# Emptying PSUM banks before the next rounding, splitting DVE's scans, and taking roots of row variances on GpSimd

## The reference, cut to what matters

```python
gq_l, gk_l, gv_l, gr_l, gaf_l, gab_l, dq_l, dk_l, dv_l = split(h_l @ w_in, IN_OFFSETS)   # and of h_c
la_f = log_sigmoid(gaf @ w_a_up_f + b_a_f) / 16      # forward gates; la_b backward
b = cumsum(la)                                        # what the scans compute
...
x_new = x + g1 * mix_l                                # output jobs out0..out3
h2_l = rms_norm(x_new, norm2_w) * (1 + sc2) + sh2
x_new = x_new + g2 * conv_ffn(h2_l, ...)              # jobs downa0..3 and downb0..3
kv = rmsnorm(mem, mem_norm_g) @ w_mem_kv              # jobs km, vm
h = rmsnorm(x, norm_g) @ w_in                         # second layer
out = rmsnorm(x + o @ w_out, final_norm_g)            # jobs o20..o23, then the end
```

## Time and profile before

| | us |
|---|---|
| median of three runs | 2324.34 (2324.21 to 2324.67) |
| the profiled execution | 2324.98 |
| its span, first to last instruction | 2323.2 |
| PE busy | 2240.4 (96% of the span) |
| DVE busy | 1485.7 (64%) |
| ACT busy | 1038.5 (45%) |
| POOL busy | 47.3 (2%) |

### The profile page before, as it was taken

How to read it: one execution, slowest core, us unless ns; L and a number is a source line. 1 busy time by engine, 2 the same in 40 slices (tenths; PEclk the granted TensorE clock), 3 DMA queues, 4 the chain that set the end, 5 groups by cost and what they waited for, 6 DMA issues and landing times.

```text
span 2323.2 us, 37359 instructions
## 1 busy us (share of the span) xinstructions
PE 2240.4 (96%) x15465; PEld 2010.0 (87%) x15465; DVE 1485.7 (64%) x2116; ACT 1038.5 (45%) x1429; POOL 47.3 (2%) x61
## 2 busy tenths in 40 slices
PE   5899999999999999989999999999999999999997
PEld 2577777899888999779999988999978898999986
DVE  3346766387476478777888855566665644576664
ACT  3134343354555643344444433444454534454444
POOL 3000000021000000000000000000000000000000
PEclk9899999999999999999999999999999999999999
DMA  9956766454444578866778655555545566544454
GB/s 364 369 163 197 230 210 197 145 151 146 127 137 129 187 243 280 293 230 206 227 243 260 225 190 190 183 185 183 185 165 196 166 189 201 170 128 137 129 198 145
DMA packets 249738, 458.75 MB, mean 197 GB/s; under 512 B 18995, under 2 KB 43889, under 8 KB 248160
## 3 DMA queue, kind: packets, MB, share of 16 engines
q1 hardware_dynamic: 246496, 442.47, 58.7%
q0 software_dynamic: 2496, 9.69, 1.1%
q10 hardware_dynamic: 576, 4.19, 0.5%
HBM read 454.20 MB, written 2.10 MB: 196 GB/s over the span
## 4 chain that ended last, share of the span: by engine, by line
PE 82%; DVE 7%; ACT 3%; DMA 3%; DVEq 2%; issue 2%; SPq 1%; ACTq 0%
PE psum L648 73%; DVE fast L1921 2%; PE psum L625 2%; DVE sbuf L1973 2%; ACT fast L1324 1%; DMA sbuf<-in_w_ada 1%; PE psum L1157 1%; DVEq L1972 1%; PE psum L904 1%; PE psum L959 1%; PE psum L719 1%; DVE fast L1941 1%; DMA sbuf<-in_w_up 1%; PE psum L978 1%; PE psum L1187 1%
## 5 line engine op out<-in xcount | busy, mean ns | idle before, releaser
L648 PE MATMUL psum<-fast,fast 128*128 128x256 f32 (+1 forms) x13424 | 2034.2, 312 | 20.6 <-DVE fast L1921 14.4
L648 PEld LDWEIGHTS psum<-fast,fast 128*128 128x128 f32 x13424 | 1848.6, 191 | 195.4 <-issue 46.6
L1921 DVE TENSOR_TENSOR fast<-sbuf,fast 128x1024 fp32r<-128x1024 f32 (+5 forms) x685 | 784.0, 1152 | 678.5 <-ACT fast L1324 671.2
L1324 ACT ACTIVATE fast<-sbuf 128x1024 fp32r<-128x1024 f32 (+4 forms) x689 | 682.1, 998 | 1046.0 <-PE psum L648 911.5
L1973 DVE SCALAR_TENSOR_TENSOR sbuf<-sbuf,sbuf 128x512 f32<-128x512 f32 x210 | 157.8, 751 | 18.3 <-issue 0.5
L1324 ACT ACTIVATE sbuf<-psum 128x512 f32<-128x512 f32 (+4 forms) x193 | 85.6, 469 | 79.9 <-PE psum L648 33.3
L625 PE MATMUL psum<-sbuf,sbuf 128*128 128x128 f32 (+2 forms) x349 | 58.7, 284 | 22.3 <-DMA sbuf<-in_consts 10.5
L625 PEld LDWEIGHTS psum<-sbuf,sbuf 128*128 128x128 f32 (+2 forms) x349 | 42.7, 145 | 33.0 <-DMA sbuf<-in_consts 10.5
L1941 DVE TENSOR_TENSOR fast<-sbuf,fast 128x512 fp32r<-128x512 f32 (+1 forms) x61 | 53.4, 876 | 4.5
L1689 ACT ACTIVATE sbuf<-psum,sbuf 128x256 f32<-128x256 f32 x88 | 44.2, 552 | 0.0
L2352 DVE SCALAR_TENSOR_TENSOR sbuf<-psum,sbuf,sbuf 128x255 f32<-128x255 f32 x88 | 38.5, 478 | 3.6 <-issue 0.4
(11 more groups left out here) (263 smaller groups left out, 962.6 us busy)
## 6 DMA issues: line engine op xcount, KB each, us to landing
sbuf<-in_w_ada SPq DMA_DIRECT2D x192, 512.0 KB, 4.9
sbuf<-in_w_up SPq DMA_DIRECT2D x176, 512.0 KB, 4.4
sbuf<-in_w_in SPq DMA_DIRECT2D x154, 512.0 KB, 3.8
sbuf<-in_w_down SPq DMA_DIRECT2D x88, 512.0 KB, 4.3
sbuf<-in_w_gate SPq DMA_DIRECT2D x64, 512.0 KB, 3.6
sbuf<-in_w_out SPq DMA_DIRECT2D x64, 512.0 KB, 4.8
sbuf<-in_w_proj_gla SPq DMA_DIRECT2D x16, 512.0 KB, 4.7
sbuf<-in_w_proj_diff SPq DMA_DIRECT2D x16, 512.0 KB, 5.9
```

What stands on the lines that cost most here:

```text
L648: last = mm(out, lhsT, rhs, start=first and key not in opened, stop=end, skip_group_check=True)
L1324: return A(out, in_, ACT.Copy, scale=scale)
L1921: last = tt(lo, raw, hi.bitcast(F32), ALU.subtract)
```

## The change

Four edits. (1) In gv0 and gv1, ACT rounds all but the last chunk of its steps, copies the four banks out, and rounds the last one then. (2) DVE's eight scans per direction are issued as four and four, with a step of the job between them; the second direction thereby begins a step later. (3) In the output and down jobs each of the two token tiles is multiplied and at once added; in out3 the last residual chunk is computed after that. (4) Four roots of row variances leave ACT: POOL computes x to the power -0.5 for norm2, mem, norm3 and the final norm. The other three, of the first norm and of the two low-rank norms, stay on ACT. POOL writes the exponent once, makes one power in advance, and its queue holds these operations between its DMAs. ACT's early Ln goes in three places.

```diff
@@ gpsimd
+            def rsqrt(x, before):
+                pool.wait_ge(S("variance_ready"), before + 1)
+                nc.gpsimd.tensor_tensor(x, x, small[:, 116:118], ALU.pow).then_inc(S("rsqrt_done"), 1)
             pool.wait_ge(S("diff_pv_done"), 8)
             pool.dma_start(g1b, dram["b_ada"][0:1, 2 * D:3 * D].to_broadcast([P, D])).then_inc(S("spread_bias"), 16)
+            pool.memset(small[:, 116:118], -0.5)
+            pool.memset(small[:, 118:120], 1.0)
+            pool.drain()
+            nc.gpsimd.tensor_tensor(small[:, 118:120], small[:, 118:120], small[:, 116:118], ALU.pow)
...
             pool.wait_ge(S("x1_slices"), 8)
             pool.dma_start(g2b, dram["b_ada"][0:1, 5 * D:6 * D].to_broadcast([P, D])).then_inc(S("spread_bias"), 16)
+            rsqrt(small[:, 58:60], 1)
+            rsqrt(small[:, 66:68], 2)
             pool.wait_ge(S("mem_ready"), 8)
...
             pool.dma_start(pev[0:32, :], dram["cmp_pe_v_2"]).then_inc(S("cmp_loaded"), 16)
+            rsqrt(small[:, 58:60], 3)
             pool.wait_ge(S("mixed2"), 8)
...
             pool.wait_ge(S("gain_loaded"), 16)
+            rsqrt(small[:, 58:60], 6)
@@ scalar
-            def steps(name):
-                for g in st.job[name]:
-                    round_chunk(st.nth[g] + 2)
+            def steps(name, left=0):
+                n = len(st.job[name]) - left
+                for q, g in enumerate(st.job[name]):
+                    if q < n:
+                        round_chunk(st.nth[g] + 2)
                     next(side, None)
...
             for j in range(2):
-                steps(f"gv{j}")
+                steps(f"gv{j}", 1)
                 for t in range(4):
                     src, emptied = filled(f"gv{j}", t)
                     copy(gv[:, t, 512 * j:512 * j + 512], src).then_inc(emptied, 1)
+                round_chunk(st.nth[st.job[f"gv{j}"][-1]] + 2)
...
-                if n == 3:
-                    logarithms_next()
...
-            rsqrt(small[:, 58:60])
...
-            rsqrt(small[:, 58:60])
-            act.drain()
+            act.wait_ge(S("rsqrt_done"), 7)
@@ vector
                             last = v.tensor_tensor_scan(dst[:, p, 1:257], C("ones")[:, 0:1].to_broadcast([P, T]),
                                                        zb[:, p, lc * T:(lc + 1) * T], 0.0, ALU.mult, ALU.add)
+                        if p == 1:
+                            yield
                     last.then_inc(S("gates_summed"), 1)
...
                     stt(otmp[:, 2 * (n % 2) + t, :], src, 0.5, gain[:, c], ALU.mult, ALU.mult).then_inc(emptied, 1)
-                dve.drain()
-                for t in range(2):
+                    dve.drain()
                     tt(x1[:, t, c], x1[:, t, c], otmp[:, 2 * (n % 2) + t, :], ALU.add).then_inc(S("x1_slices"), 1)
...
             for n in range(4):
-                steps(f"out{n}")
+                steps(f"out{n}", n // 3)
                 add_rows(f"out{n}", n, g1b, "g1_kept")
+            rest_chunk(st.nth[st.job["out3"][-1]] + 2)
```

More of the change, by code:

```diff
@@ L1319, in _ @@
             A = nc.scalar.activation
-            roots = 0
             side = iter(())
@@ L1349, in filled, with rsqrt @@
                 return bank(BANKS[name][i]), S(f"bank_emptied{BANKS[name][i]}")
[L1351 to L1354, removed]
+            def rsqrt(v, before):
+                act.wait_ge(S("variance_ready"), before + 1)
                 A(v, v, ACT.Ln)
@@ L1373, in _ @@
                 act.drain()
-            rsqrt(small[:, 12:16])
+            rsqrt(small[:, 12:16], 0)
             rows_copy(0)
@@ L1649, in squares @@
                       ).then_inc(S("x1_squared"), 1)
-            def logarithms_next():
-                A(small[:, 84:85], small[:, 7:8], ACT.Ln)
             for n in range(4):
                 steps(f"out{n}")
-                if n == 3:
-                    logarithms_next()
                 squares(0, n)
@@ L1731, in mem_units @@
                     yield
-                rsqrt(small[:, 66:68])
                 for _ in range(6):
@@ L1795, in second_block @@
                     if step in (26, 30):
-                        rsqrt(lowrs[:, step // 4 - 6, :])
+                        rsqrt(lowrs[:, step // 4 - 6, :], step // 4 - 2)
                     if step == 42:
@@ L1922, in rest_chunk, with steps @@
                 last.then_inc(S("weights_split"), 1)
-            def steps(name):
-                for g in st.job[name]:
-                    rest_chunk(st.nth[g] + 2)
+            def steps(name, left=0):
+                n = len(st.job[name]) - left
+                for q, g in enumerate(st.job[name]):
+                    if q < n:
+                        rest_chunk(st.nth[g] + 2)
                     modulation(st.nth[g])
```

## The result

| us | before | after |
|---|---|---|
| median | 2324.28 (4 runs, 2322.65 to 2324.67) | 2308.47 (4 runs, 2305.73 to 2309.00) |
| profiled execution, its span | 2324.98, 2323.2 | 2309.00, 2307.2 |
| stops of PE that the prediction reckoned with: gv0 to gv1, gv1's last chunk, gv1 to dk0 | 2.30, 1.23, 2.02 | none |
| ahead of norm2, in downb1, ahead of norm3 | 6.07, 3.30, 1.47 | 4.60, 1.68, none |
| wait for the final root | 1.82 | 0.90 |

The ratio is 0.9929, with a 95% interval of 0.9917 to 0.9941. That is 15.8 us by the medians (13.7 to 19.3 by the interval).

A forecast was written before the change was run, and what follows sets the result against it. A TensorE (PE) matmul stream, 82% of the last chain, with short stops, was taken to bound the kernel. 5.55 - 0.13 + (0.46 + 1.22) + 1.7 + 1.47 + 1.22 = 11.5 us, giving 2312.8; range 2310.5 to 2318.2.

The forecast's parts named there:

- Mem: Inside downb0 and downb1: root on POOL removes DVE's 1.84 wait, less 0.13 for tile order; 1.7 us gained.
- Banks and scans: Values jobs, gv0 to dk0: PE's three stops of 2.30, 1.23 and 2.02 go; 5.55 us gained at best, 0 at worst.
- The power: 0.6: POOL's power replacing ACT's root: wait of 0.6 us in all, hand-overs included, within bounds of 0.2 to 2.5.
- norm2's and the final root: Ahead of norm2 and at the kernel's end: DVE's wait falls from 1.82 to 0.6; 1.22 us gained at each.
- Rivals 2 and 3: Power waits of about 3 us: about 2320, chance 0.07; or each power restarting POOL's code: 2330.8, chance 0.05.
- the bound of 2.2: Ahead of norm3: PE's 1.47 stop goes as long as the power takes under about 2.2 us.
- Norm3: Ahead of norm3: the rounding queued behind ACT's exponential runs earlier, so PE's stop goes; 1.47 us gained.
- Norm2's share of edit 3: End of out3 into norm2: variance starts at about 1027.34, not 1027.80; 0.46 us gained.
- Tile by tile: Output tiles, where PE waits behind ACT's squares once after out0: one more drain; 0.13 us lost.
- rivals 1 and 4: dk0 stays where it is: 2316.1, chance 0.12; or PE finds the next chunk late at both boundaries: 2318.4, chance 0.05.

The follow-up runs named there:

- late squares: ACT's squares of an output or down job issued behind the next job's third rounding, against the changed kernel (the kernel after): 2305.51 us, ratio 0.9917 to the kernel before.

## Why the prediction fell short, step by step

- **Mem: the step that failed.** The sum priced every stop of PE by its idle time alone. For mem I took 1.7 us, for a stop of 3.30 that shrinks to 1.6. The stop did shrink to 1.68, but the term was worth 3.2 in the trace (3.0 to 7.2 timed alone), since the clock behind it no longer falls. The evidence was in the trace that I had: 36 matmuls take 8.77 in out3, and the 36 behind the stop of the earlier trace rows took 10.18, in a row that I did not quote. The same mistake is in the bank term below. With mem at 3.2 and the banks at 6.66 the sum is 14.1 and the forecast 2310.2, 1.7 above what was measured; the rest is what no term had, the start and the pauses, less what was taken too high.
- **Banks and scans.** "5.55 at best" was no upper bound. In the very trace that I used the part is worth 6.66 (restarts), and where the first stop is a little longer it is 8.8 to 9.1. The chain of causes was right as far as it went: the load was late because DVE held the slot. I then treated the late copies as the cause to be cured, and did not count that splitting the scans cures the load itself.
- **The power: 0.6.** It takes 0.69 to 0.72, and DVE's wait is 0.84 ahead of norm2 and 0.90 at the end, inside the bounds; norm2's and the final root are worth 0.98 and 0.91, not 1.22. Rivals 2 and 3 did not happen. The one power that took longer (1.61 to 1.62 ahead of norm3, in each of the eight traces that have it) was hidden, as the bound of 2.2 said. The 0.6 was a guess between bounds and a lucky one: no row showed a power.
- **Norm3.** 1.47 forecast, 1.54 found, no stop left.
- **Norm2's share of edit 3.** 0.46 forecast, 0.50 found.
- **Tile by tile.** 0.13 forecast for out0, 0.17 found there (1.72 against 1.55 with edit 3 alone); 0.18 and 0.16 more appear in downb1 and ahead of norm3 where the roots stay on ACT.
- **Later stages (rivals 1 and 4).** Nothing came back: dk0 starts with no stop, and the offset of 8.4 to 8.5 us holds to out0.
- **Not forecast: DVE's pauses, 1.01.** From norm3 to the end the kernel before has pauses of 0.43 us on DVE that nothing in the profile releases. Three of the four between 2079 and 2226 reach PE: at two of them the offset of the two kernels grows, by 0.29 and 0.34, and the last makes the stop at o20 1.70, where it is 1.34 after.

```profile
2079.57 0.17 DVE L2532 TENSOR_REDUCE sbuf<-sbuf 128x1 f32<-128x15 f32 x1 [0.43 <-issue]
...
2225.61 0.43 DVE L1939 CAST fast<-sbuf 128x512 fp32r<-128x512 f32 x1 [0.43 <-issue]
```

All six traces without edit 3 have the same four, at the same operations. Those with edit 3 have two, at others: 2030.48 and 2147.99 in the kernel after, and at the same operations in the run with edit 3 alone and in that with late squares. The one and three operations added at mem moved them again. So the pauses seem to hang on where an operation stands in DVE's stream of instructions, which edit 3 lengthens by some drains, and not on what it does; that fits all fourteen traces but is not tested by itself. What makes them the runs don't show.
- **Not forecast: the start, 1.80.** No edit touches the code ahead of the first mark, and in fourteen traces it falls between 185.31 and 189.25. It is chance and belongs to no edit.

The parts as the traces have them are 6.7 to 9.1 for banks and scans, -0.6 up to out3, 1.5 at norm2, 3.2 at mem, 1.5 at norm3, 1.0 for the pauses and 0.9 at the end: 14.2 to 16.6 us. The 15.8 that was measured lies inside, without the start. Of the -0.6 the tile order explains 0.2; in the trace with edits 1 and 2 alone the stretch is 0.44 longer than before as well, so the rest is likely not edit 3's. In the six traces without edit 3 this stretch goes from 754.37 to 757.90 us, most of it by the clock behind the stop ahead of out0, so that single traces and single runs leave 1 to 3 us open.

## What to carry to other kernels

Price a stop of PE not by its bracket but by the marks around it: compare the block behind the stop with a block of the same matmuls elsewhere, and look at its granted clock. Where several stops follow one late load, ask first what gives the load's slot back; the later repairs may be redundant. One trace is one sample: a stop that does not bring the clock down in it may do so in the next, and the other way round, and the range should hold both.

## What the runs showed of the hardware

- From gv0 on, the clock stayed at 1.00 behind all of PE's stops of 1.0 to 2.46 us. Behind the six stops of 3.30 to 3.48 in downb1 it fell, and 36 matmuls took 9.99 to 11.30 us instead of 8.6; behind the waits of 4.59 to 6.07 ahead of norm2 it was 0.50 to 0.60 in all fourteen traces. In between both were seen: no fall at 2.51, a fall at 2.53, 2.57 and 2.63; and of the twelve stops of 3.14 to 3.20 ahead of out0 nine with a fall and three without (96 matmuls in 23.6 to 24.9 us against 22.0). Ahead of gv0, where PE waits again and again for w_ada, the clock was low behind much shorter stops (0.52 behind one of 1.51). The Trainium skill, "TensorE: Matmul & The Clock Gate", section "What's actually happening", says that the unit that sets the clock runs free of the kernel, so that the moment of a change varies. These runs agree: 2.51 without and 2.53 with a fall, 3.20 without and 3.14 with one.
- DVE pauses of 0.43 us stay at the same operation from run to run and move when instructions are added ahead of them.
- A `drain` on POOL right behind a load that POOL issued took 8.8 to 9.9 us in nine traces and ended 1.4 to 1.5 us after that load had landed.
- A power of 128x2 on POOL takes 0.69 to 0.75 us, but 1.61 to 1.62 ahead of norm3 in every trace and once 1.27; from variance to the first scaled rows it is about 1.0 where Ln, a table load and Exp on ACT took 2.0.
